# Single-pass products for the down slots of two dense layers, VectorE for the remainders of one, and two norms with one round of sums

## The reference, cut to what matters

```python
def rms_norm(x, g):
    y = x * lax.rsqrt(jnp.mean(x * x, axis=-1, keepdims=True) + EPS)
    return y * g
mod = silu(c) @ w_ada + b_ada                # six vectors of 1024 a layer
h = rms_norm(x, norm_g) * (1.0 + scale) + shift
x = x + gate * mixer(h)
h = rms_norm(x, norm_ffn_g) * (1.0 + scale_f) + shift_f
x = x + gate_f * feed_forward(h)
```

## Time and profile before

| | us |
|---|---|
| median of 3 runs | 2569.79 (2569.15 to 2570.77) |
| the profiled execution | 2563.78 |
| its span | 2562.0 |
| TensorE busy | 2496.2 (97%) |
| VectorE busy | 1773.8 (69%) |
| ScalarE busy | 1199.0 (47%) |
| GpSimd busy | 333.2 (13%) |

### The profile page before, as it was taken

The page is one execution under the profiler, slowest core; times in us unless marked ns, Lnnn a source line. Parts: engine busy times, 40 slices in busy tenths (PEclk is TensorE's granted clock), DMA queues, the critical chain, the costliest instruction groups (busy, mean ns, idle before and its releaser), DMA issues.

```text
span 2562.0 us, 36960 instructions
## 1 busy us (share of the span) xinstructions
PE 2496.2 (97%) x14304; PEld 2170.4 (85%) x14304; DVE 1773.8 (69%) x1949; ACT 1199.0 (47%) x1273; POOL 333.2 (13%) x97
## 2 busy tenths in 40 slices
PE   5999999999999999999999999898999999999999
PEld 4889998878888888888888888788999899998998
DVE  5832775768888888888888888455379788873112
ACT  3213213117667676767676767322312356663221
POOL 0005550000000000000000000001344200002552
PEclk8999999999999999999999999999999999999999
DMA  8745884766989898989898989330478543442442
GB/s 365 316 164 206 347 318 183 301 246 252 363 321 363 322 362 318 363 320 362 321 363 318 362 321 362 124 136 17 160 306 316 227 165 135 146 148 99 166 175 86
DMA packets 90383, 656.18 MB, mean 256 GB/s; under 512 B 10032, under 2 KB 10288, under 8 KB 10800
## 3 DMA queue, kind: packets, MB, share of 16 engines
q1 hardware_dynamic: 80928, 589.34, 60.9%
q10 hardware_dynamic: 9360, 65.52, 6.4%
HBM read 653.76 MB, written 1.05 MB: 256 GB/s over the span
## 4 chain that ended last, share of the span: by engine, by line
PE 72%; issue 17%; POOL 6%; DVE 3%; ACT 1%; ACTq 0%; DMA 0%; POOLq 0%; DVEq 0%; SPq 0%
PE bank L1164 71%; POOL ring_rounded L737 6%; PE bank L1709 1%; DVE work L1862 1%; DVE rstd L1910 0%; DVE xT L1856 0%; DMA ring<-stream_dram 0%; DVE ring L1862 0%; PE bank L1533 0%; DVE ring_rounded L1850 0%; DVE yT L1856 0%; ACTq L758 0%; ACT work_rounded L778 0%; POOL work L697 0%; PE bank L1635 0%
## 5 line engine op out<-in xcount | busy, mean ns | idle before, releaser
L1850 DVE TENSOR_TENSOR ring_rounded<-ring,work_rounded 128x2048 fp32r<-128x2048 f32 x372 | 842.3, 2290 | 159.4 <-ACT work_rounded L912 122.1
L1164 PE MATMUL bank<-work_rounded,proj_rounded 128*128 128x512 f32 x1792 | 614.3, 406 | 0.6 <-DVE proj_rounded L1850 0.2
L912 ACT ACTIVATE work_rounded<-ring 128x2048 fp32r<-128x2048 f32 x224 | 428.5, 1914 | 0.0
L1164 PEld LDWEIGHTS bank<-work_rounded,proj_rounded 128*128 128x128 f32 x1792 | 338.0, 189 | 76.9 <-issue 2.9
L1164 PE MATMUL bank<-ring_rounded,proj_rounded 128*128 128x512 f32 x896 | 353.6, 395 | 0.0
L1164 PE MATMUL bank<-work_rounded,ff_hid_rounded 128*128 128x512 f32 x896 | 302.3, 398 | 1.8 <-DVE ff_hid_rounded L1850 1.8
L1164 PE MATMUL bank<-yT_rounded,ring_rounded 128*128 128x256 f32 x960 | 271.6, 283 | 0.0
L1164 PE MATMUL bank<-hT,ring 128*128 128x256 f32 x1088 | 243.3, 384 | 1.1 <-ACT hT L802 1.1
L1164 PEld LDWEIGHTS bank<-hT,ring 128*128 128x128 f32 x1088 | 208.1, 192 | 36.4 <-issue 8.6
L1164 PE MATMUL bank<-ff_hid,ring 128*128 128x256 f32 x1056 | 232.9, 379 | 0.0
L1164 PEld LDWEIGHTS bank<-ff_hid,ring 128*128 128x128 f32 x1056 | 198.4, 190 | 25.9
(11 more groups left out here) (286 smaller groups left out, 4299.5 us busy)
## 6 DMA issues: line engine op xcount, KB each, us to landing
ring<-stream_dram SPq DMA_DIRECT2D x561, 1024.0 KB, 4.8
work<-stream_dram ACTq DMA_DIRECT2D x56, 1024.0 KB, 9.1
params<-params_dram ACTq DMA_DIRECT2D x1, 1728.5 KB, 28.6
consts<-consts_dram ACTq DMA_DIRECT2D x1, 1568.0 KB, 37.5
cond<-cond_dram ACTq DMA_DIRECT2D x2, 512.0 KB, 3.8
xT<-x_dram ACTq DMA_DIRECT2D x1, 1024.0 KB, 10.4
out_dram<-xT SPq DMA_DIRECT2D x1, 1024.0 KB, 3.9
consts<-consts_dram ACTq DMA_DIRECT2D x1, 577.0 KB, 32.0
```

The source lines that it names most:

```text
L912: act.activation(up_high[u][half], ring[:, (moe_first + s + half) % RING, :], ACT.Copy)\
L1164: return pe.matmul(o, lhsT=a, rhs=b, start=start, stop=stop, skip_group_check=True)
L1850: return dve.tensor_tensor(o, a, b, op)
```

## The change

The down slots of all chunks but the last, in layers 1 and 4, go in three single passes like the up slots. That needs a third high copy and a third remainder a chunk (two more high buffers, `ff_down_high`), and a high and a low part of the hidden tile `ff_hid`: ScalarE copies it (`hid_high`), VectorE subtracts (`hid_low`), TensorE waits for the latter. In layer 1 all three remainders of a chunk are computed by VectorE, none by GpSimd. In layer 4 GpSimd computes all three. Layer 3 keeps its two split slots a chunk on GpSimd and its float32 down slots. In all three dense layers `high(c, odd, 0)` now stands ahead of `load_modulation`. VectorE's modulation is cut into one block and two blocks, with `hidden_low` and the third remainder between them. The tile `cond` moves behind `h_heads` in SBUF. GpSimd waits for the end of layer 1's feed-forward before layer 2's mixers.

The norm of the final norm is computed from the same `x`: TensorE sums x² and x²g² in one go, VectorE works out the second mean as `sum * rstd * rstd`, and the normed `x` itself is written after the tiles of the next mixer's input.

```diff
+SPLIT_DOWN = ("first0", "odd")
+LOWS_ON_DVE = ("first0",)
...
+        split_buffers = [w_high[0], w_high[1], ff_down_high[0], w_high[2], w_high[3], ff_down_high[1]]
+        down_split = [kind in SPLIT_DOWN for kind in plan]
+        split_width = [3 if split else 2 for split in down_split]
...
@@ GpSimd, first_mixers @@
                 if n:
                     pool.wait_ge(mod_part, parts_before(n + 1))
+                    pool.wait_ge(weights_used, place[f"in{n}"])
+                    pool.wait_ge(split_low, splits_before[n])
...
@@ GpSimd, feed_forward @@
-                with pool.Fori(0, SPLITS // PAIR_SPLITS) as i:
-                    for r in range(PAIR_SPLITS):
-                        low(r, i * PAIR_SPLITS + r)
+                if plan[n] not in LOWS_ON_DVE:
+                    with pool.Fori(0, (DENSE_CHUNKS - 1) // 2) as i:
+                        for r in range(2 * width):
+                            low(r, i * (2 * width) + r, split_buffers[r // width * 3 + r % width])
...
@@ ScalarE, norm @@
+                if follows_final(u):
+                    act.wait_ge(*final_vec.at("mean", 0))
+                    act.activation(twice_mean, twice_mean, ACT.Sqrt, bias=EPS, scale=1.0 / D)\
+                       .then_inc(norm_act.sem, KD + 1)
+                    norm_act.count += KD + 1
...
@@ ScalarE, feed_forward, visit @@
+                    if not final:
+                        high(c, odd, 0)
                     if n + 1 < len(plan) and not isinstance(c, int):
                         load_modulation(n + 1, c - 2)
-                    if not final:
-                        high(c, odd, 0)
                     if isinstance(c, int) and c == 0:
                         high(c, odd, 1)
                     tiles(c, odd)
                     if not (isinstance(c, int) and c == 0) and not final:
                         high(c, odd, 1)
+                    if down_split[n] and not final:
+                        act.wait_ge(ffn_hid, base + 2 * c + 2)
+                        if not isinstance(c, int) or c >= 2:
+                            act.wait_ge(weights_used, c * 3 + (first - 1))
+                        act.activation(ff_hid_high[:, 2 * odd:2 * odd + 2, :], ff_hid[:, 2 * odd:2 * odd + 2, :], ACT.Copy)\
+                           .then_inc(hid_high, 1)
+                        high(c, odd, 2)
...
@@ TensorE, norm @@
+                if follows_final(u):
+                    return
...
+                if which == 2:
+                    for k in range(KD):
+                        pe.wait_ge(*norm_vec.at(f"s{k}", u))
+                        last = mm(bank(5, 0, T), const("ones"), yT[:, k, :], k == 0, k == KD - 1)
+                    last.then_inc(*norm_pe.step("sum"))
...
@@ TensorE, down @@
+                        q = splits + 3 * c + 3
+                        pe.wait_ge(split_low, q if i is None else i * 6 + q)
+                        parts = [p.rearrange("p (j n) -> p j n", j=2)
+                                 for p in (ff_down_high[c % 2], ring_r[:, (first + 3 * c + 4) % RING, :])]
+                        t = hid_before[n] + c + 1
+                        pe.wait_ge(hid_low, t if i is None else i * 2 + t)
...
+                                last = mm3(o, [p[:, j, d * P:d * P + P] for p in parts],
+                                           (ff_hid_high[:, b, :], ff_hid_low[:, b, :]), start, False)
...
@@ VectorE @@
+            def final_norm(u):
+
+                n = norms[u][0]
+                dve.wait_ge(*norm_vec.at("s7", u - 1))
+                dve.wait_ge(*x_ready(u))
+                tt(gain_sq, norm_gain(n, 2), norm_gain(n, 2), ALU.mult).then_inc(*final_vec.step("sq"))
+                dve.tensor_copy(gain[:, :], norm_gain(n, 2)).then_inc(*norm_vec.step("gain"))
+                dve.wait_ge(*final_vec.at("sq", 0))
+                for k in range(KD):
+                    stt(yT[:, k, :], xT[:, k, :], gain_sq[:, k:k + 1], xT[:, k, :], ALU.mult, ALU.mult)\
+                        .then_inc(*norm_vec.step(f"s{k}"))
+                root_inverse(u)
+                dve.wait_ge(*norm_rstd.at("rstd", u))
+                dve.wait_ge(*norm_pe.at("sum", u + 1))
+                tt(twice_mean, bank(5, 0, T), rstd[:, :], ALU.mult).then_inc(*final_vec.step("scaled"))
+                dve.wait_ge(*final_vec.at("scaled", 0))
+                tt(twice_mean, twice_mean, rstd[:, :], ALU.mult).then_inc(*final_vec.step("mean"))
+
+            def norm_of_normed(n, u):
...
+                dve.wait_ge(*norm_act.at("root", u))
+                dve.reciprocal(twice_mean, twice_mean).then_inc(*norm_rstd.step("rstd"))
+                dve.wait_ge(*norm_rstd.at("rstd", u))
+                tt(twice_mean, twice_mean, rstd[:, :], ALU.mult).then_inc(*final_vec.step("root"))
...
+                for k in range(KD):
+                    stt(yT[:, k, :], xT[:, k, :], gain_both[:, k:k + 1], twice_mean, ALU.mult, ALU.mult)\
+                        .then_inc(*norm_vec.step(f"s{k}"))
+                dve.wait_ge(*norm_vec.at("s7", u))
+                for k in range(KD):
+                    last = stt(xT[:, k, :], xT[:, k, :], gain[:, k:k + 1], rstd[:, :], ALU.mult, ALU.mult)
+                last.then_inc(*final_vec.step("x"))
...
@@ VectorE, feed_forward, visit @@
+                    weights_low(0)
                     for j in range(2):
...
                         tt(ff_hid[:, b, :], bank(4 + b, T, 2 * T), ff_silu[:, b, :], ALU.mult).then_inc(ffn_hid, 1)
-                    if n + 1 < len(plan) and not isinstance(c, int):
-                        mod_parts(n + 1, c - 2, range(MOD_GROUP))
+                    weights_low(1)
+                    modulate(range(1))
+                    hidden_low()
+                    if down_split[n]:
+                        weights_low(2)
+                    modulate(range(1, MOD_GROUP))
```

More of the change, by code:

```diff
@@ L206, in build_program @@
         h_heads = sb("h_heads", shapes["h_heads"])
+        cond = sb("cond", [P, D])
         xT = sb("xT", [P, KD, T])
@@ L366, in build_program @@
         h_low = pflat_r[:, SLOT:2 * SLOT].rearrange("p (k t) -> p k t", k=KD)
-        assert mod_at >= 2 * SLOT
+        ff_down_high = [work_r[:, mod_at + (MOD_GROUP + u) * SLOT:mod_at + (MOD_GROUP + 1 + u) * SLOT] for u in range(2)]
+        assert mod_at >= 2 * SLOT and mod_at + (MOD_GROUP + 2) * SLOT <= work_n - D
+        ff_hid_high, ff_hid_low = (rounded["h_heads"][:, a * 4 * T:(a + 1) * 4 * T].rearrange("p (b t) -> p b t", b=4)
+                                   for a in range(2))
         weights_here = [sem(f"weights_here{i}") for i in range(RING)]
@@ L385, in build_program @@
         norm_rstd = steps("norm_rstd", "rstd")
+        final_vec = steps("final_vec", "sq scaled mean gain root x")
+        twice_mean, gain_sq, gain_next, gain_both = (
+            ff_mid[:, 0, :], *(ff_mid[:, 1, a * KD:(a + 1) * KD] for a in range(3)))
         norm_vec = steps("norm_vec", "gain " + " ".join(f"s{k}" for k in range(KD)))
@@ L554, in build_program, with follows_final @@
             norms += [(n, 0), (n, 1)] + ([(n, 2)] if kind == "first1" else [])
+        def follows_final(u):
+            return u > 0 and norms[u - 1][1] == 2
         def x_ready(u, k=KD - 1):
@@ L727, in feed_forward @@
             def feed_forward(n):
-                first, before = place[f"ffn{n}"] + 2, dense_before[n] * SPLITS
+                first, before, width = place[f"ffn{n}"] + 2, splits_before[n], split_width[n]
                 pool.wait_ge(*high_act.at("h", dense_before[n]))
@@ L783, in norm @@
                     act.wait_ge(x_here, 16)
-                for k in range(KD):
+                for k in range(0 if follows_final(u) else KD):
                     if u:
@@ L1216, in norm @@
                 else:
-                    keep_running(14 if plan[n] == "odd" and which == 0 else 7)
+                    keep_running(14 if plan[n] == "odd" and which == 0 else 7, 0 if which == 2 else 5)
             def normed(n, which, k):
@@ L1796, in down @@
                 def down(c, i=None, final=False):
[L1797 to L1801 removed]
+                    plain = final or not down_split[n]
+                    if plain:
+                        at = ff_down(first, c, chunks)
+                        arrive(at, i)
+                        t = base + 2 * c + 2
+                        pe.wait_ge(ffn_hid, t if i is None else i * 4 + t)
+                    else:
+                        q = splits + 3 * c + 3
[4 more added lines that the diff above has]
+                        pe.wait_ge(hid_low, t if i is None else i * 2 + t)
                     for j in range(2):
@@ L1925, in norm @@
             def norm(n, which):
                 u = norms.index((n, which))
+                if which == 2:
+                    return final_norm(u)
+                if follows_final(u):
+                    return norm_of_normed(n, u)
                 if which == 0:
@@ L1944, in norm @@
                 for k in range(KD):
```

(21 more changed lines are left out.)

67 lines of the change are left out of this document (37 added, 30 removed).

## The result

The changed kernel takes 2546.47 us (median of 4 runs, 2544.66 to 2548.62), the kernel before, beside it, 2569.47 (4 runs, 2565.51 to 2570.77). The ratio is 0.9914, interval 0.9901 to 0.9927: 22 us faster, 19 to 25. The profiled execution took 2544.66 us, with a span of 2542.9, against 2563.78 before: 19.1 less. I had put 14.9 on that difference.

A forecast was written before the change was run, and what follows sets the result against it. TensorE, busy for 97% of the span, was taken as the bound. Terms -13.7 - 11.4 + 11.8 - 1.6 = -14.9 us took the median from 2569.8 to 2554.9 us, range 2542 to 2563 (8 times in 10).

The forecast's parts named there:

- the forecast's own 2550 to 2561: Whole kernel: range of the forecast case alone, with the third layer between +7 and +15.5 us; chance 0.65.
- the 6.0 us from before: Whole kernel: the median of the runs was taken to lie 6.0 us above the profiled execution.
- rival A: Third layer: it doesn't lose, its loop staying under 18.42 us without exclusion; whole 2543 or 2538 us; chance 0.14.
- First layer, -13.7 forecast: Layer 1 runs at TensorE's 17.28 us a chunk: -11.4 us, and its 2.3 us of waits go.
- Rival B: First layer: VectorE becomes the bound, giving 4 us back; whole 2559 us; chance 0.10.
- Fourth layer, -11.4 forecast: Layer 4's split downs gain 11.4 us; GpSimd's 14.3 us of work fit in 17.28 a chunk.
- the gain of a chunk: Down slots, first and fourth layers: 48 passes at 0.12, 5.76 us, replace a 6.90 us float32 down, saving 1.14.
- Rival C: Down slots: passes run slower as every third changes the PSUM tile, from 0.136 us on; whole 2578 us; chance 0.05.
- Third layer, +11.8 forecast: Layer 3: the earlier high copy makes GpSimd's remainders alternate with dot products; waits of 16.6 us against 4.8 before.
- the loop: 20.9 us, not 21.2: Third layer: a visit's alternating dot products and remainders close in 21.2 us, against 19.5 before and TensorE's 18.42.
- Norms, -1.6 forecast: Norms after layer 2: the second round leaves the chain, so the second norm's products start 1.6 us earlier (0 to -3).
- Rival D: Norms: they don't shorten, since the pause before the next products lasts as long; 2556 us; within the forecast's chance 0.65.

The follow-up runs named there:

- old_order_everywhere: Changed kernel with the modulation DMAs ahead of the first high copy again in layers 1, 3 and 4: 2546.18 us, ratio to the kernel before 0.9918.
- first_gpsimd_remainders: Changed kernel, but in layer 1 GpSimd instead of VectorE subtracts all three remainders of a chunk: 2604.49 us, ratio 1.014.
- split_fourth_alone: Kernel before, with layer 4's downs split (cut modulation, GpSimd's layer 2 waits and place of `cond` stay as changed): 2554.36 us, ratio to before 0.9944.
- third_short_dots: Changed kernel, but layer 3's dot products on VectorE read only 64 of 1024 columns, leaving out most of layer 4's modulation: 2534.86 us, ratio 0.9874.
- old_norms: Changed kernel with the two norms after layer 2 in full, one after the other, as before the change: 2551.49 us, ratio to before 0.9931.
- old_order_third: Changed kernel with the first high copy back behind the modulation's DMAs in layer 3 alone: 2540.42 us, ratio to before 0.9894.

## Why the prediction was right, point by point

The forecast was 2554.9 us, the time is 2546.5: inside the range of 2542 to 2563, but below the forecast's own 2550 to 2561. Of those 8.4 us, 4.2 are in the terms (19.1 in place of 14.9, each profiled execution against the other). The others come from where a profiled execution stands to its median: I took the 6.0 us from before, and after it was 1.8. By the time alone rival A (2543) would have been nearer than my 2554.9. What decides for the forecast is the third layer's stretch, which got longer by 9.8 us. That the time still fell inside the range is in part the width of a range that reached to A: all four terms erred to the same side, and so did the median.

**First layer, -13.7 forecast, -14.6 measured.** Its waits are gone. Rival B made VectorE the bound; it isn't, and B falls. `old_order_everywhere` shows how near it stood: with the first copy behind the modulation's DMAs the loop is 18.6 us and 6.2 are lost. That it is GpSimd's absence which lets the dot products run is shown by `first_gpsimd_remainders`: +51 us.

**Fourth layer, -11.4 forecast, -12.4 measured.** `split_fourth_alone` has it by itself. In both layers the step that was mis-sized is the gain of a chunk, 1.14 us forecast and 1.23 measured: 6.91 for the float32 down against 5.68 for 48 passes at 0.118, not 0.12. Rival C needed 0.136 a pass or more and falls: a change of the PSUM tile every third pass costs nothing that can be seen. Three single passes take 5.68 / 6.73 = 0.84 of a float32 product's time. The count of four passes for float32 (the Trainium skill, FP8 and Floating Point Precision, TensorE Precision Notes), read as a ratio of times, would make it 0.75 and a down 5.2 us; the rows don't bear that out, and the measurement decides.

**Third layer, +11.8 forecast, +9.8 measured.** The mechanism is shown: the alternation of a dot product and a remainder, and the loop above TensorE's pace from chunk 4 on. Rival A falls with it. The term that was mis-sized is the loop: 20.9 us, not 21.2. TensorE waited six times, as in my sum, and six times 0.3 is 1.8 of the 2.0 us between forecast and stretch. The starts of the downs are 20.8 to 20.9 us apart from down(3) to down(7), 2.3 to 2.5 over TensorE's 18.42.

I had no term for the clock. After the fifth wait TensorE's granted clock fell to 1.2 GHz, from 1988.1 to 1991.5 us (the window of this row starts 0.5 us earlier, hence its 0.56), and two passes followed each other at 0.21 us:

```profile
1987.60:1991.00 3.40, 3.40 (x20) 3.40 (x19) 3.40 (x1) 0.00 (x0) 3.40 (x1) 0.56 0.69 287
```

```profile
1989.19 0.41 PE L1197 MATMUL bank<-yT_rounded,ring_rounded 128*128 128x256 f32 x1
1989.40 0.41 PE L1197 MATMUL bank<-yT_rounded,work_rounded 128*128 128x256 f32 x1
```

The down behind it started 22.35 us after the one before, 1.5 more than the loop. But the stretch didn't get longer by it, since the next wait for GpSimd took the 1.5 us back: it was 0.75 us long in place of 2.2. GpSimd had kept its pace (1981.03, then 2001.83), and TensorE went on when its second remainder was done, at 2007.4:

```profile
2001.83 5.58 POOL L756 TENSOR_TENSOR ring_rounded<-ring,proj_rounded 128x2048 fp32r<-128x2048 f32 x1 [9.81 <-ACT proj_rounded L1127]
```

```profile
2007.46 0.38 PE L1197 MATMUL bank<-yT_rounded,proj_rounded 128*128 128x256 f32 x1 [0.75 <-POOL ring_rounded L756]
```

So leaving the clock out did the sum no harm here: where a helper engine sets the pace, a slow TensorE costs only what the next wait can't give back.

Who holds up whom: the dot product that began first ran at its own 1.22 us, the remainder behind it took 5.48 and the next dot product 5.57, and with dot products of 64 columns the remainders are back at 4.6. The Trainium skill (SBUF — State Buffer, Who interferes with whom) states that a VectorE instruction with two SBUF inputs contends with a GpSimd instruction that reads SBUF, and that the order of issue decides who blocks. These rows agree.

**Norms, -1.6 forecast.** On TensorE it is 20.8 us before and 18.9 after from the first sum to the first product of the next projections, -2.0 (from the first square 23.3 and 19.7, -3.6). But the clock falls at different places in the two. A like pair is `split_fourth_alone` with the old norms and `third_short_dots` with the new ones. TensorE in the first:

```profile
1638.38 5.41 PE L1200 MATMUL bank<-hT,consts 128*128 128x256 f32 x16 [2.58 <-ACT hT L808]
...
1654.22 6.80 PE L1200 MATMUL bank<-params,hT 128*128 128x8 f32 x32 [0.28 <-ACT hT L829]
1660.87 3.35 PE L1200 MATMUL bank<-hT,ring 128*128 128x256 f32 x8
```

and in the second:

```profile
1619.69 5.15 PE L1197 MATMUL bank<-hT,consts 128*128 128x256 f32 x16 [2.67 <-ACT hT L807]
1624.67 3.62 PE L1197 MATMUL bank<-yT,consts 128*128 128x256 f32 x16
...
1633.15 6.53 PE L1197 MATMUL bank<-params,hT 128*128 128x8 f32 x32 [1.74 <-ACT hT L828]
1639.54 4.81 PE L1197 MATMUL bank<-hT,ring 128*128 128x256 f32 x13
```

The first sum and the small matmuls are slow in both. From the first sum to the first projection it is 22.5 and 19.9 us, -2.6, within my 0 to -3. The products of the second norm start 14.8 us after the first sum in the one and 12.4 in the other, -2.4, where I had -1.6. `old_norms` against the changed kernel, with half-clock stretches at other places again, has 23.9 and 18.9 us. The first square stands 2.5 us ahead of the first sum in the one and 1.5 in the other, which makes 1.0 us more; why is open. Rival D falls by this pair. The 8 products of the first norm, moved behind the next input's tiles, stop nobody.

**The rest.** By TensorE's timeline the terms are -14.6, -12.4, +9.8 and -2.0 for the norms, -19.2, and the whole is -19.1. What lies between them nearly cancels: up(1) of the first layer starts 0.3 us later, the part from the first layer's end to the norms' first sum is 0.7 shorter, and the part from the first projection behind the norms to the third layer's up(1) is 0.5 longer. Ahead of layer 2's experts TensorE runs at half clock in three places both before and after, 20.4 and 20.5 us together, though at other lengths (10.2, 6.8 and 3.4 us before; 13.7, 3.4 and 3.4 after). In `old_order_third` the part between the first sum after layer 1 and the norms' first sum is 1233.5 us against 1229.6, with the same code. Half-clock stretches that are longer together make 1.7 of these 3.9; the rest is open. No term of a sum can foresee this from the diff, and it is why I compare stretches and not medians where they differ by a few us.

## What to carry to other kernels

Before moving an operation to relieve one wait, ask what its successor will then run beside: here a copy made earlier sent two GpSimd subtractions into VectorE's dot products, and a chunk became 2.4 us longer than TensorE needs. Where VectorE works on operands that lie in SBUF, give it the remainders too if it has room; two of them cost it 4.6 us a chunk and gave back the 8.9 that two dot products had lost (5.6 each in place of 1.15), and that kernel runs in 2535.0 us, 0.987 of before. Here a float32 product that was cut into three single passes took 16% less time, so it pays only where no helper engine sets the pace: in the third layer, with VectorE's 19.4 us a visit, it gave nothing.

## What was not expected of the hardware

- A single pass of 256 columns costs 0.118 us in the downs and 0.12 in the ups (why is open), and the first pass behind a float32 product costs 0.30. At the granted clock of 1.2 GHz a pass costs 0.21.
- A short operation suffers as much as a long one from GpSimd's subtraction: the hidden remainder is 0.68 us alone, and 4.97 beside it in layer 1 (`first_gpsimd_remainders`). In the fourth layer VectorE's busy time went from 36.0 us to 82.3 with ten of them, up to 4.7 each, and TensorE never waited.
- The granted clock fell to 1.2 GHz for 3.4 us in the third layer after five waits of 2.1 to 2.3 us, and not once in that stretch of the kernel before, where five waits of 0.4 to 0.8 us stood. The 1.5 us that it cost were gone again after the next wait.
